# A two-layer trunk on one core: ScalarE's skip-tap copies, the scan's outputs and the turned activations in another order

## The reference

```python
def s5_mixer(h, w_in, lam_re, lam_im, log_dt, b_re, b_im, c_re, c_im, d_skip, w_glu):
    u = (h @ w_in).astype(jnp.float32)
    ...
    lam_bar = jnp.exp(lam * dt)
    b_bar = ((lam_bar - 1.0) / lam)[..., None] * b_c
    def chunk_step(state, u_c):
        bu = jnp.einsum('bcgh,gph->bcgp', u_c.astype(jnp.complex64), b_bar)
        a_cum, x_loc = lax.associative_scan(_scan_op, (a, bu), axis=1)
        xs = x_loc + a_cum * state[:, None]
        y = jnp.real(jnp.einsum('bcgp,ghp->bcgh', xs, c_c))
        return xs[:, -1], y
    ...
    y = y.transpose(1, 0, 2, 3, 4).reshape(bsz, seq, D_MODEL) + d_skip.astype(jnp.float32) * u
    g = jax.nn.gelu(y).astype(h.dtype)
    val, gate = jnp.split(g @ w_glu, 2, axis=-1)
    return val * jax.nn.sigmoid(gate)
```

## Time and profile before

| What | Value |
|---|---|
| median of three runs | 790.54 us |
| the three runs | 789.68 to 792.15 us |
| the profiled execution's own time | 791.36 us |
| its span in the trace | 789.6 us |
| PE busy | 682.4 us (86%) |
| DVE busy, ACT busy | 299.4 us (38%), 249.2 us (32%) |
| mean granted TensorE clock | 0.954 of full |

### The profile page before, as it was taken

The page is one execution under the profiler, slowest core; times in us unless marked ns, Lnnn a source line. Parts: engine busy times, 40 slices in busy tenths (PEclk is TensorE's granted clock), DMA queues, the critical chain, the costliest instruction groups (busy, mean ns, idle before and its releaser), DMA issues.

```text
span 789.6 us, 16128 instructions
## 1 busy us (share of the span) xinstructions
PE 682.4 (86%) x6390; PEld 403.8 (51%) x6404; DVE 299.4 (38%) x776; ACT 249.2 (32%) x579; POOL 35.3 (4%) x36
## 2 busy tenths in 40 slices
PE   4898999989977577576899999898989999985994
PEld 4787654555534244244444444555655655652562
DVE  6899761171111011011232534736334433331334
ACT  6687433261111011011311314534233322321224
POOL 1770000000000000000000000000000000000000
PEclk9999999999998887899999999999999999997998
DMA  9335609879999999999990565048999933999981
GB/s 251 112 134 193 186 8 412 346 299 381 419 421 419 422 420 420 422 420 409 381 382 22 213 220 206 0 172 327 424 419 421 420 163 114 423 419 421 419 336 54
DMA packets 64767, 237.92 MB, mean 301 GB/s; under 512 B 24432, under 2 KB 24640, under 8 KB 40128
## 3 DMA queue, kind: packets, MB, share of 16 engines
q1 hardware_dynamic: 63808, 236.82, 75.8%
q10 hardware_dynamic: 896, 0.24, 0.1%
HBM read 235.21 MB, written 1.84 MB: 300 GB/s over the span
## 4 chain that ended last, share of the span: by engine, by line
PE 55%; SPq 15%; DMA 12%; DVE 10%; ACT 5%; issue 2%; DVEq 0%; ACTq 0%
SPq L437 12%; PE ps L1901 12%; PE ps L1992 10%; PE ps L1956 6%; PE ps L1816 6%; PE ps L1881 5%; DMA hT<-in_moe_w_up 4%; DMA ring<-in_moe_w_up 4%; PE ps L1921 4%; DMA ring<-in_moe_w_down 3%; SPq L435 2%; PE ps L2055 2%; PE ps L2066 2%; ACT work L730 2%; PE ps L1964 1%
## 5 line engine op out<-in xcount | busy, mean ns | idle before, releaser
L1901 PE MATMUL ps<-ring,work 128*32 128x256 f32 x1504 | 125.7, 418 | 35.8 <-DMA ring<-in_moe_w_up 12.6
L1901 PEld LDWEIGHTS ps<-ring,work 128*32 128x32 f32 x1504 | 70.6, 120 | 77.9 <-issue 57.6
L1901 PE MATMUL ps<-work 128*32 128x256 f32 x864 | 90.4, 412 | 18.6 <-DMA ring<-in_moe_w_up 6.1
L1433 DVE TENSOR_TENSOR work<-ps,work 128x256 f32<-128x256 f32 x21 | 12.9, 614 | 190.9 <-PE ps L1901 190.9
L1956 PE MATMUL ps<-ring,work 128*32 128x512 f32 x464 | 70.7, 611 | 6.5 <-issue 5.8
L1901 PEld LDWEIGHTS ps<-work 128*32 128x32 f32 x864 | 49.2, 119 | 49.7 <-issue 33.0
L1881 PE MATMUL ps<-work,xr 128*128 128x128 bf16 x736 | 66.4, 219 | 0.7 <-DVE work L1342 0.6
L1881 PE MATMUL ps<-work 128*128 128x128 bf16 x368 | 63.9, 219 | 0.0
L1881 PEld LDWEIGHTS ps<-work,xr 128*128 128x128 bf16 x736 | 57.6, 98 | 8.9 <-issue 3.3
L1992 PE MATMUL ps<-ring,hT 128*128 128x512 f32 x128 | 58.1, 608 | 1.8 <-ACT hT L646 1.8
L1816 PE MATMUL ps<-ring,work 128*128 128x512 f32 x128 | 56.2, 595 | 0.9 <-ACT work L730 0.5
(11 more groups left out here) (338 smaller groups left out, 1070.5 us busy)
## 6 DMA issues: line engine op xcount, KB each, us to landing
ring<-in_moe_w_down SPq DMA_DIRECT2D x22, 2048.0 KB, 24.1
ring<-in_moe_w_gate SPq DMA_DIRECT2D x21, 2048.0 KB, 19.6
ring<-in_moe_w_up SPq DMA_DIRECT2D x16, 2048.0 KB, 30.2
work<-in_moe_w_up SPq DMA_DIRECT2D x12, 2048.0 KB, 20.7
work<-in_moe_w_gate SPq DMA_DIRECT2D x9, 2048.0 KB, 28.9
work<-in_moe_w_down SPq DMA_DIRECT2D x8, 2048.0 KB, 23.8
ring<-in_ssm_w_glu SPq DMA_DIRECT2D x4, 2048.0 KB, 9.0
ring<-in_attn_w_qkv SPq DMA_DIRECT2D x4, 2048.0 KB, 27.5
```

The source lines that it names most:

```text
L1901: ins = mm(ps[s, 6 + j // 2, 0:256], xg[:, k, s], pairs[slots[e // 2]][e % 2][:, k, :], start=(k == 0), stop=(k == KD - 1))
```

## The change

It removes no arithmetic and adds none. It moves four things.

First, `own(0)`, sixteen copies in one piece on ACT, is cut by time offset. Offset 0 goes ahead of `keep_u(3)`, offset 1 behind the last `keep_w1T`, and offsets 2 and 3 behind `keep_x(2)`. For that, `taps(0)` and `taps(1)` on PE move ahead of `turn_w1(3, 0)` and `inputs(7)`, and `skips(0)` on DVE moves ahead of `carries(0)`. Second, `skips(1)` moves from ahead of `carries(1)` to its middle. Third, `y` is cut in two, `y_taps` and `y_states`, and the turns and slices of `glu` are written between the pieces. Fourth, on ACT `keep_g(0)` comes ahead of `gelu(1)`.

```diff
-            def own(half):
+            def own(half, js=range(SB)):
...
-                for j in range(SB):
+                for j in js:
...
             spread_w2(5)
+            keep_w1T(3, 0)
+            own(0, (0,))
             keep_u(3)
-            keep_w1T(3, 0)
+            keep_w1T(3, 1)
+            own(0, (1,))
             keep_x(2, (0, 1))
-            keep_w1T(3, 1)
-            own(0)
+            own(0, (2, 3))
             keep_x(3, (0, 1))
...
             gelu(0)
+            keep_g(0)
             gelu(1)
-            keep_g(0)
             keep_g(1)
...
                 for h in range(1, SEG - 1):
+                    if half and h == 4:
+                        skips(1)
                     advance(at(h + 1), at(h), mu4[:, :, :, 1, rs])
...
-                else:
-                    skips(1)
+                    skips(0)
                 carries(half)
                 if half == 0:
-                    skips(0)
                     dve.wait_ge(u_done, 8)
...
             turn_w1(2, 1)
-            inputs(7)
-            turn_w1(3, 0)
-            drive(2)
-            turn_w1(3, 1)
             taps(0)
             taps(1)
+            turn_w1(3, 0)
+            inputs(7)
+            turn_w1(3, 1)
+            drive(2)
             drive(3)
...
-            y(0)
-            y(1)
+            y_taps(0)
+            y_states(0)
+            y_taps(1)
             turn_g(0)
+            y_states(1)
+            glu(0, range(2))
             turn_g(1)
-            glu(0, range(4))
+            glu(0, range(2, 4))
             taps(2)
             taps(3)
             glu(2, range(4))
             pe.wait_ge(f_ready, 32)
-            glu(1, range(4))
-            y(2)
-            y(3)
+            glu(1, range(2))
+            y_taps(2)
+            y_states(2)
+            glu(1, range(2, 4))
             turn_g(2)
+            y_taps(3)
+            y_states(3)
+            glu(0, range(4, 6))
             turn_g(3)
-            glu(0, range(4, KD))
+            glu(0, range(6, KD))
             glu(2, range(4, KD))
             glu(1, range(4, KD))
```

More of the change, by code:

```diff
@@ L1772, in _, with rows, y_taps @@
             turn_w1(2, 1)
-            inputs(7)
-            turn_w1(3, 0)
-            drive(2)
-            turn_w1(3, 1)
             taps(0)
             taps(1)
+            turn_w1(3, 0)
+            inputs(7)
+            turn_w1(3, 1)
+            drive(2)
             drive(3)
[L1781 to L1787, removed]
+            across = [4 * (n % 2) + n // 2 for n in range(OCT)]
+            def rows(o, r):
+                h = r // 4
+                return ps[64 * h:64 * h + 64, o, P * (r % 4):P * (r % 4) + P]
+            def y_taps(o):
                 pe.wait_ge(f_ready, 16 if o < 2 else 32)
@@ L1790, in y, with y_states @@
                 for r in across:
-                    mm(rows(r), U4[:, OCT * o + r, :], Fw[:, OCT * o + r, :], start=(r % 4 == 0), stop=False, skip_group_check=True)
+                    mm(rows(o, r), U4[:, OCT * o + r, :], Fw[:, OCT * o + r, :], start=(r % 4 == 0), stop=False, skip_group_check=True)
+            def y_states(o):
                 pe.wait_ge(state, o + 1)
@@ L1794, in y @@
                     for r in across:
-                        ins = mm(rows(r), Xs[o][:, i, r, :], W2[:, i, OCT * o + r, :], start=False, stop=(i == 1),
+                        ins = mm(rows(o, r), Xs[o][:, i, r, :], W2[:, i, OCT * o + r, :], start=False, stop=(i == 1),
                                  skip_group_check=True)
```

## The result

The changed kernel takes 793.67 us (median of 18 runs, 792.48 to 796.49) against 791.52 us for the kernel before (18 runs beside it, 788.45 to 795.66). The ratio is 1.0035, with a 95% interval of 1.0022 to 1.0049: slower by 1.7 to 3.9 us, best estimate 2.8. As a change, +0.25 us was forecast; about 1 us of the distance in absolute times is the base, since the forecast was added to a median of three runs, 790.54 us. The profiled execution took 793.05 us, its span 791.3.

What follows compares the result with a forecast made beforehand. PE was taken to bound the kernel up to about 140 us, its shifts reaching the end. 1.6 - 1.8 + 0.7 - 0.25 = +0.25 us gave a 790.8 us median, no measurable change; 8-in-10 range 788.0 to 793.2.

Steps and rivals of the forecast that it cites:

- The moved pause: PE's 3.83 us wait ahead of `y(0)` moves ahead of `drive(3)`, as 3.6 us waiting for the restack's transfers.
- the steps: Reckoning from taps at 60.07 us: later `inputs(7)`, copies ahead of `keep_u(3)`, restack write at 68.4, landing at 74.6.
- What the clock costs there: Low clock in `drive(3)` costs 1.9 us, so outputs start at 80.1 instead of 78.52 us: +1.6 us.
- the nearest row: Profile row of the kernel before: clock at 0.50 for 3.75 us behind a like pause, half of it counted lost.
- then run at full clock: Both octets' outputs after `drive(3)` take 5.4 us in place of 7.27: -1.8 us.
- fall as a whole: Prediction fails if the 60 to 140 us stretch changes by over 2.4 us, or its shift misses the end.
- Rival 1: Clock stays low through `drive(3)` and into the outputs, back after about 83 us: +2.95, 793.5 us; chance 0.20.
- Turns and projection: Interleaving outputs, turns and `glu`: first two turns 2.55 us against 1.82, +0.7; octets 2 and 3, -0.25.
- the forecast wait behind the second turn: PE waits about 1.4 us for ACT's copies behind the second turn, before the next piece of `glu`.
- The second half: Octets 2 and 3: interleaving replaces 2.7 us, including the 1.55 us pause, by 2.45: -0.25 us.
- Part three: `skips(1)` inside `carries(1)`, `keep_g(0)` first: about 2.4 us leaves the path to the last states, counts nothing.
- Covers and pass-through: Remaining `own(0)` pieces and projection weights (4 us cover) come in time; shifts before 140 us reach the end whole.

Runs made afterwards that it cites:

- e5_keepu: Changed kernel with `keep_u(3)` back ahead of the first piece of `own(0)` on ACT: 793.76 against 791.74 us, ratio 1.0031.
- e6_inputs_first: Changed kernel with `inputs(7)` and `turn_w1(3, 0)` back ahead of the taps, `keep_u(3)` first on ACT: 791.16 against 791.74 us, ratio 0.9997.
- e3_fill_after: Changed kernel with four idle wide products between `drive(2)` and `drive(3)`: 791.21 against 791.88 us, ratio 0.9999.
- e10_wide_first: Changed kernel with four idle wide products after the wait for the restacked inputs, ahead of `drive(3)`: one run, 794.84 us.
- e2_back: Kernel before plus interleaved outputs, turns and `glu`, `skips(1)` in the carries, `keep_g(0)` first; `own(0)` uncut: 790.76 against 791.88 us, ratio 0.9986.
- e1_front: Only the cut of `own(0)`, with early taps and `skips(0)`; the rest as in the kernel before: 795.48 against 791.88 us, ratio 1.0050.
- e7_hidden: e6_inputs_first with other PE work behind each second turn and two `spread_w2` ahead of `keep_g(1)`: 789.58 against 791.74 us, ratio 0.9974.
- e8_hidden_fill: e7_hidden with two idle wide products between `drive(3)` and the outputs: 790.68 against 791.74 us, ratio 1.0006.
- e4_fill_before: Kernel before with four idle wide products between `drive(3)` and `y(0)`: 790.65 against 791.88 us, ratio 0.9981.
- e9_best: e7_hidden with one idle wide product ahead of `drive(3)`, two behind, `skips(1)` ahead of `carries(1)` again: 787.88 against 791.26 us, ratio 0.9954.

## Why the prediction was wrong

**The moved pause: right.** SP's write of the restack was issued at 67.73 + 0.67 = 68.40, forecast 68.4. The pause was 3.84 us, forecast 3.6, and was ended by the transfer into `gains`. `drive(3)` began at 74.92, forecast 74.6. e5_keepu and e6_inputs_first show that its two causes are those in the steps: the taps ahead of `inputs(7)` and the copies ahead of `keep_u(3)`.

**What the clock costs there: the step that failed.** The prediction took "the nearest row, the 3.75 us behind a pause of the same length in the same stage: 1.9 us" and had the outputs "then run at full clock", -1.8. In fact `drive(3)` took 7.06 us instead of 3.6, a loss of 3.46. The outputs started at 81.24 + 0.67 = 81.91 instead of 78.52: +3.39 where +1.6 was forecast. They ran at half rate almost through the first octet, and took 89.09 - 81.24 less 0.58 for the turn between, 7.27 us, just as before: 0 where -1.8 was forecast. These two terms are 1.8 + 1.8 = 3.6 us of the forecast's error, and the stage lengthened by 4.04 us, over the 2.4 at which the prediction was to fall as a whole. The row was chosen by the length of the pause, but what differed was the work behind it: outputs of 128 columns there, `drive`'s 64 columns here. e3_fill_after shows that the clock is the cause: same wait for the same transfer, clock 1.00, no loss. e10_wide_first shows, in one run, that the work behind the pause decides when the clock is back. The other profiles bear it out: in the eight in which the clock fell in this stage, it was back 3.7 to 4.1 us after work resumed where outputs or wide products stood there (the kernel before, e2_back, e10_wide_first), and 10.3 to 11.4 us after where `drive(3)` did (the changed kernel, e1_front, e5_keepu, e7_hidden, e8_hidden_fill). Counted from the first product behind `drive(3)`, that is 3.5 to 4.6 us in these five.

The Trainium skill, "TensorE: Matmul & The Clock Gate", section "What's actually happening", has it that activity releases the low clock. The changed kernel agrees only in part: 6.99 us in which PE counts as fully busy passed at 0.50, while in e10_wide_first the clock was back after 4 us of other products.

**Rival 1 was what happened, and in the stage dearer.** It was given 0.20 and 793.5 us. Its sign held: the clock came back after 83 us (84.8 + 0.67 = 85.5). It counted 3.6 us for `drive(3)` and 1.0 for the outputs; the outputs lost all of 1.8, so in the stage the price was 4.04 rather than 2.95. That the median lies only 0.2 us from 793.5 is partly luck: the whole kernel shows less than the stage, and the median before, to which it is held, lay 1 us higher than the one that rival 1 started from. The argument for it, that products of 64 columns may not count for much, stood in the text and was outweighed by the clock's staying at 1.00 through `drive(2)`. That showed only that the clock had not fallen while `drive(2)` ran, not that its products raise a low one.

**Turns and projection: right within half a microsecond.** The first two turns cost 0.58 + (94.38 - 92.63) = 2.33 us for 1.82, +0.5 (forecast +0.7), with the forecast wait behind the second turn (1.15 us; 1.4 was named). From there to the wait for `own(1)` it was 16.76 us for 16.64, +0.1. The second half, 107.60 to 143.38, is 35.78 us for 35.76: 0.0 where -0.25 was forecast. The sum 3.39 + 0 + 0.5 + 0.1 + 0.0 is 4.0, the stage's 4.04. Part three shows nothing in the changed kernel, as forecast; no run tests it alone.

**Covers and pass-through: right.** `own(0)` did not hold PE, nor did the projection's weights. The stage's shift arrived: from the last row of the stage to the first gate product it was 34.09 us before and 34.03 after, and the DMA queue stood still at 178 to 180 us.

**What stays open.** The stage says +4.0 us and the whole kernel's ratio says +2.8 (1.7 to 3.9). Later stretches that the change does not touch vary by clock falls of their own, below; how much of the 1.2 us between is such chance, the runs don't settle.

## What to carry to other kernels

Before taking a wait away, follow what feeds the next waiter: here the work moved forward pushed a transfer out and back through HBM late by as much as the wait removed. Price a pause of PE not by its length alone but by the work that follows it, and look in the rows for that same work behind a pause before using a duration. Where a pause cannot go, some wide products of idle work ahead of it, or in it, held the clock here (e3_fill_after, e4_fill_before, e9_best); behind it they cost more than they gave (e8_hidden_fill, e10_wide_first).

## What the runs showed of the chip that I had not expected

- **The same products, either side of the clock.** `drive`'s sixteen products passed at 1.00 when the clock was there (3.68 us in `drive(2)`) and left it at 0.50 for their whole 7 us when it was not (the changed kernel, e1_front, and nearly so e8_hidden_fill). Whether it is their columns or their weight loads, which fill PEld for 6.87 of 6.99 us, no run separates.
- **The clock can fall behind a pause of 0.6 us.** With the same order on PE up to `drive(3)`, e6_inputs_first kept 1.00 over a pause of 0.46 us and one of 1.55, while e7_hidden and e8_hidden_fill lost it with 0.65 and 0.60. With wide products ahead, e3_fill_after kept it over 0.69. In all eight falls of this stage a `drive` and then a pause stood just ahead, and in seven the fall came 0.7 to 1.2 us after that `drive` had ended, whether PE then stood still for 0.6 us or for 3.8; in e5_keepu it came 3.6 us after. So the length of the pause is not what the falls have in common, but e6_inputs_first had the same work and no fall. Each is one execution; what decides, or whether chance does, is open.
- **Steps of about 1.5 us in code that nobody changed.** From the end of the projection to the first gate product, the same code in all twelve profiles, it took 34.0 to 34.1 us in six, 35.5 to 35.6 in four and 37.2 in two. The granted clock goes with it: from 155 to 180 us it was 1.00 in those six, 0.93 in the four and 0.86 in the two. Here are e9_best and e3_fill_after:

```profile
155.00:180.00 25.00, 23.81 (x255) 15.72 (x256) 14.63 (x71) 11.57 (x24) 0.00 (x0) 0.93 0.70 273
```

```profile
155.00:180.00 25.00, 22.45 (x178) 13.73 (x181) 15.04 (x72) 14.44 (x31) 0.00 (x0) 0.86 0.66 253
```

One or two such steps are as large as the effects studied here, and they are why the stage's rows, not a single execution's total, carry the attributions above.
